# Second homes for five of an expert quad's twelve weight units, loops over two quads

## The reference, cut to what matters

```python
def hier_moe(hn, w_grp, w_exp, w_gate, w_up, w_down):
    ...
    e_in = jnp.einsum('ng,nge->ne', jax.nn.one_hot(grp, N_GROUPS, dtype=jnp.float32), e_logits)
    top_p, top_i = lax.top_k(jax.nn.softmax(e_in, axis=-1), TOP_K_IN_GROUP)
    gate = p_g * top_p / jnp.sum(top_p, axis=-1, keepdims=True)
    expert = grp[:, None] * EXPERTS_PER_GROUP + top_i.astype(jnp.int32)
    ...
    def expert_block(args):
        xb, e = args
        hh = jax.nn.silu(xb @ w_gate[e]) * (xb @ w_up[e])
        return hh @ w_down[e]
```

## Time and profile before

| | us |
|---|---|
| median of 3 runs | 1954.98 |
| lowest and highest run | 1954.23, 1959.61 |
| the profiled execution, its own time | 1956.8 |
| span of the profiled execution | 1954.9 |
| busy: PE, PEld, DVE, ACT, POOL | 1732.8, 1263.4, 864.2, 627.6, 60.0 |

### The profile page before, as it was taken

One profiled execution on the slowest core, in us unless ns is written; L12 is line 12 of the kernel. 1 busy time (PEld: TensorE's weight loads), 2 busy tenths in 40 slices (PEclk: granted clock), 3 DMA queues, 4 the chain that ended last, 5 costly groups with the idle time before them and its releaser, 6 DMA issues.

```text
span 1954.9 us, 31288 instructions
## 1 busy us (share of the span) xinstructions
PE 1732.8 (89%) x12626; PEld 1263.4 (65%) x12626; DVE 864.2 (44%) x1528; ACT 627.6 (32%) x1021; POOL 60.0 (3%) x58
## 2 busy tenths in 40 slices
PE   7999778788788899988878888899999989999997
PEld 7985334344245768543433433599888979998897
DVE  5642122122125644212212212469876555987654
ACT  4421111111113642201101111364447554543763
POOL 0200000000000010000000000100001200000110
PEclk9999998898898999988989989999999999998999
DMA  7638999999998313899999999544522334442222
GB/s 299 235 149 344 421 422 421 421 422 421 421 421 346 127 44 151 358 421 421 421 421 422 421 421 422 206 166 135 191 88 102 103 117 149 154 172 103 93 89 106
DMA packets 73091, 526.35 MB, mean 269 GB/s; under 512 B 8241, under 2 KB 8497, under 8 KB 9265
## 3 DMA queue, kind: packets, MB, share of 16 engines
q1 hardware_dynamic: 73008, 525.18, 67.3%
HBM read 524.10 MB, written 1.05 MB: 269 GB/s over the span
## 4 chain that ended last, share of the span: by engine, by line
PE 52%; DMA 27%; DVE 8%; SPq 7%; ACT 3%; issue 2%; POOL 0%; DVEq 0%; ACTq 0%
DMA arena<-experts 19%; PE banks L453 13%; PE banks L457 10%; PE banks L458 9%; PE banks L459 9%; SPq L412 7%; DMA ring<-experts 5%; PE banks L612 4%; PE banks L597 3%; PE banks L630 3%; DMA ring<-dense 2%; DVE arena L1429 2%; DVE ring_parts L1409 1%; DVE hT L1560 1%; ACT ring_parts L1016 1%
## 5 line engine op out<-in xcount | busy, mean ns | idle before, releaser
L457 PE MATMUL banks<-arena_parts,ring_parts 128*128 128x256 f32 (+1 forms) x1444 | 426.0, 295 | 28.0 <-DVE arena_parts L1424 13.2
L458 PE MATMUL banks<-arena_parts,ring_parts 128*128 128x256 f32 (+1 forms) x1444 | 415.1, 287 | 0.0
L459 PE MATMUL banks<-arena_parts,ring_parts 128*128 128x256 f32 (+1 forms) x1444 | 414.9, 287 | 0.0
L453 PEld LDWEIGHTS banks<-arena 128*128 128x128 f32 (+3 forms) x2704 | 342.9, 201 | 76.8 <-issue 60.9
L453 PE MATMUL banks<-arena 128*128 128x128 f32 (+5 forms) x2704 | 378.7, 298 | 13.4 <-DVE arena L1555 5.0
L1016 ACT ACTIVATE arena<-banks 128x256 f32<-128x256 f32 (+9 forms) x350 | 159.3, 485 | 462.4 <-PE banks L453 205.6
L457 PEld LDWEIGHTS banks<-arena_parts,ring_parts 128*128 128x128 f32 x1444 | 279.1, 193 | 39.5 <-issue 18.3
L1409 DVE TENSOR_TENSOR ring_parts<-ring,ring_parts 128x1024 fp32r<-128x1024 f32 x204 | 244.1, 1238 | 125.8 <-ACT ring_parts L1016 123.9
L612 PE MATMUL banks<-ring,arena 128*32 128x512 f32 x1536 | 210.3, 656 | 94.3 <-DMA ring<-experts 90.9
L458 PEld LDWEIGHTS banks<-arena_parts,ring_parts 128*128 128x128 f32 x1444 | 280.2, 194 | 0.1
L459 PEld LDWEIGHTS banks<-arena_parts,ring_parts 128*128 128x128 f32 x1444 | 279.5, 194 | 0.0
(11 more groups left out here) (208 smaller groups left out, 1614.2 us busy)
## 6 DMA issues: line engine op xcount, KB each, us to landing
ring<-experts SPq DMA_DIRECT2D x192, 1024.0 KB, 26.2
arena<-experts SPq DMA_DIRECT2D x160, 1024.0 KB, 20.8
ring<-dense SPq DMA_DIRECT2D x112, 1024.0 KB, 4.9
at<-experts SPq DMA_DIRECT2D x32, 1024.0 KB, 22.8
consts<-consts_in SPq DMA_DIRECT2D x1, 1414.0 KB, 13.7
vecs<-vecs_in SPq DMA_DIRECT2D x1, 1125.5 KB, 16.1
hT<-h_in SPq DMA_DIRECT2D x2, 544.0 KB, 4.6
out<-x SPq DMA_DIRECT2D x4, 256.0 KB, 2.3
```

What stands on the lines that cost most here:

```text
L453: return pe.matmul(o, lhsT, rhs, start=(k == 0), stop=(k == n - 1))
L457: pe.matmul(o, lhsT[0], rhs[0], start=(k == 0), stop=False)
L458: pe.matmul(o, lhsT[0], rhs[1], start=False, stop=False)
L459: return pe.matmul(o, lhsT[1], rhs[0], start=False, stop=(k == n - 1))
```

## The change

Units 7 to 11 get a second home, which the odd quads of a layer use; units 0 to 6 keep one home. Three of the second homes are floats 0 to 6144 of `arena`, unit 11's is floats 6144 to 8192 (over the start of `mo_n`), unit 10's is `x2`. SP issues units 7 to 11 of quad 1 right behind units 0 to 5 of quad 0, during the routing; unit 10 waits for `lg_done`, unit 11 (and what follows it in the list) for `xr_done`. From then on SP goes by turns: units 0 to 6 of quad j + 1, each when quad j has used it, then units 7 to 11 of quad j + 2, each when quad j has used it and when quad j + 1's has landed. At the end the order differs: units 0 to 6 of the last quad come before its units 7 to 11. The loops of SP and TensorE have two quads in a turn; VectorE computes the numbers for them with two more small operations; VectorE's and ScalarE's loops still go quad by quad.

```diff
+TWICE = 7
@@
-        n_iter = sb("n_iter", [P, 2], I32)
+        n_iter = sb("n_iter", [P, 4], I32)
@@
+        second_slots = arena[:, 0:4 * UNIT].rearrange("p (s n) -> p s n", n=UNIT)
+
+        def expert_slot(u, odd=False):
+
+            if odd and u >= TWICE:
+                return x2_flat[:, 0:UNIT] if u == 10 else second_slots[:, 3 if u == 11 else u - TWICE, :]
             if u < RING:
                 return ring[:, u, :]
             return more_slots[:, u - RING, :] if u < QU - 1 else at_flat[:, :]
@@
-        a = Place(3 * DC * T)
+        a = Place(4 * UNIT)
         g_squares, root_x = a(DC, P), a(SEQ)
@@
                 experts_first(layer, range(RING))
+                sp.wait_ge(pr_done, 8 * layer + 8)
+                for u in range(TWICE, QU):
+                    if u == 10:
+                        sp.wait_ge(route["lg_done"], layer + 1)
+                    if u == 11:
+                        sp.wait_ge(route["xr_done"], layer + 1)
+                    sp.wait_ge(m[f"landed{u}"], 16)
+                    sp.dma_start(expert_slot(u, True), experts[layer, 1, u]).then_inc(m[f"landed{u}"], 16)
+
+                def is_used(pair, odd, u):
+
+                    sp.wait_ge(m["used"], pair * (2 * QU) + (odd * QU + u + 1))
+
+                def next_quad(pair, odd):
+
+                    for u in range(TWICE):
+                        is_used(pair, odd, u)
+                        sp.dma_start(expert_slot(u), experts[layer, (pair * 2 + (odd + 1 + QUADS)) % QUADS, u]).then_inc(m[f"landed{u}"], 16)
+
+                def quad_but_one(pair, odd):
+
+                    for u in range(TWICE, QU):
+                        is_used(pair, odd, u)
+                        sp.wait_ge(m[f"landed{u}"], (pair * 2 + (odd + 2)) * 16)
+                        sp.dma_start(expert_slot(u, odd == 1), experts[layer, (pair * 2 + (odd + 2)) % QUADS, u])\
+                          .then_inc(m[f"landed{u}"], 16)
+
                 sp.wait_ge(route["iter_ready"], layer + 1)
-                last = sp.value_load(n_last[0:1, layer:layer + 1], min_val=QUADS - 1, max_val=QUADS * ROUNDS - 1)
+                last = sp.value_load(n_last[0:1, layer:layer + 1], min_val=QUADS // 2 - 2, max_val=QUADS * ROUNDS // 2 - 2)
                 with sp.Fori(0, last) as i:
-                    for u in range(QU):
-                        sp.wait_ge(m["used"], i * QU + (u + 1))
-                        sp.dma_start(expert_slot(u), experts[layer, (i + 1) % QUADS, u]).then_inc(m[f"landed{u}"], 16)
+                    for odd in range(2):
+                        next_quad(i, odd)
+                        quad_but_one(i, odd)
+                next_quad(last, 0)
+                quad_but_one(last, 0)
+                next_quad(last, 1)
+                next_quad(last + 1, 0)
+                quad_but_one(last, 1)
@@
-                with pe.Fori(0, n) as i:
+                def quad(i, odd):
...
-                        return expert_slot(u).rearrange("p (e n) -> p e n", e=4)
+                        return expert_slot(u, odd).rearrange("p (e n) -> p e n", e=4)
...
-                combine(n)
+
+                with pe.Fori(0, half) as pair:
+                    quad(pair * 2, False)
+                    quad(pair * 2 + 1, True)
+                combine(half * 2)
@@
-                ts(r_c, r_n, -1.0, ALU.add)
+                ts(r_c, r_n, 0.5, ALU.mult)
+                t.link(v.tensor_copy(n_iter[:, 2 + layer:3 + layer], r_c))
+                ts(r_c, r_c, -2.0, ALU.add)
                 t.link(v.tensor_copy(n_last[:, layer:layer + 1], r_c))
                 t.link(v.tensor_copy(n_iter[:, layer:layer + 1], r_n), route["iter_ready"])
```

More of the change, by code:

```diff
@@ L413, in load_experts @@
+                next_quad(last, 0)
[3 more added lines that the diff above has]
+                quad_but_one(last, 1)
                 for u in range(QU):
-                    use = (m["used"], last * QU + (u + 1))
+                    use = (m["used"], last * (2 * QU) + (3 * QU + u + 1))
                     if u < RING:
@@ L601, in moe @@
                 pe.wait_ge(route["iter_ready"], layer + 1)
-                n = pe.value_load(n_iter[0:1, layer:layer + 1], min_val=QUADS, max_val=QUADS * ROUNDS)
-                with pe.Fori(0, n) as i:
+                half = pe.value_load(n_iter[0:1, 2 + layer:3 + layer], min_val=QUADS // 2, max_val=QUADS * ROUNDS // 2)
+                def quad(i, odd):
                     def weights(u):
                         pe.wait_ge(s[f"landed{u}"], i * 16 + 16)
-                        return expert_slot(u).rearrange("p (e n) -> p e n", e=4)
+                        return expert_slot(u, odd).rearrange("p (e n) -> p e n", e=4)
                     pe.wait_ge(s["xs_ready"], i + 1)
@@ L625, in moe @@
                     pe.wait_ge(s["ht_ready"], i + 1)
-                    for half in range(2):
+                    for half_ in range(2):
                         for k in range(2):
-                            w = weights(8 + 2 * half + k)
+                            w = weights(8 + 2 * half_ + k)
                             for e in range(4):
-                                m = pe.matmul(psum[32 * e:32 * e + 32, 4 + half, :], mo_ht[:, k, 32 * e:32 * e + 32], w[:, e, :],
+                                m = pe.matmul(psum[32 * e:32 * e + 32, 4 + half_, :], mo_ht[:, k, 32 * e:32 * e + 32], w[:, e, :],
                                               start=(k == 0), stop=(k == 1), tile_position=(0, 32 * e))
                             m.then_inc(s["used"], 1)
-                combine(n)
+                with pe.Fori(0, half) as pair:
+                    quad(pair * 2, False)
+                    quad(pair * 2 + 1, True)
+                combine(half * 2)
             def mla():
```

2 lines of the change are left out of this document (1 added, 1 removed).

## The result

| | before | changed |
|---|---|---|
| median of 10 runs, us | 1958.8 | 1948.2 |
| profiled execution: own time, span | 1956.8, 1954.9 | 1945.9, 1943.9 |
| ratio, 95% interval | | 0.9948 (0.9932 to 0.9964) |
| busy PE, PEld, DVE, ACT | 1732.8, 1263.4, 864.2, 627.6 | 1730.5, 1256.7, 866.1, 627.4 |

The changed kernel is 0.52% faster, 10.2 us of 1958.8 (7.1 to 13.3). Forecast were 13.1 us and 1942, range 1936 to 1950. One of the ten executions of the changed kernel took 2010.8 us at a granted clock of 0.82 (the other nine 0.92 to 0.94); it is in the median of the table and not in the ratio. Single executions of one kernel lie 1% apart here (before: 1948.8 to 1968.6 in 30 runs of a later group), so what follows reads stages within traces.

The account below looks back on a forecast made before the run. The prediction took the 421 GB/s stream of expert weights, with a hole in each routing, to bound the kernel. Gains of 5.2 and 7.9 us made 13.1, from 1954.98 to 1942 us; its own range 1939 to 1944, overall 1936 to 1950.

Parts of the forecast that it names:

- What bounds the kernel: Both layers of experts: a stream of 1 MB units at the DMA's full rate, 421 GB/s, 2.49 us a unit.
- The hole: Expert weight stream rests during each layer's routing, 8.9 and 9.5 us; five preloaded units, 12.4 us of stream, close it.
- The end order: Layer ends: TensorE's work on the last two quads exceeds 19.9 us of stream, so layer 0 gains 4.9 to 5.8, not 8.9.
- Its size: Gain at the layer ends: 5.2 us in layer 0 (4.9 to 5.8), 7.9 in layer 1 (7.1 to 8.9).
- the one for unit 6, unit 7 and the rest of quad 14: TensorE late in each layer: unit 6 0.86 to 1.80 us, then to quad 15 16.24 (layer 0), 15.31 to 16.24 (layer 1).
- The full clock behind a quad that did not wait: Layer 1, `prep` to last `combine`: 15.58 us instead of 16.32, 0.7 us gained.
- VectorE's operations, the waits of SP, the branch: Routing and expert loops: operations and SP's waits cost nothing; branch gone between quads 14 and 15, below 0.1 us either way.
- The doubled body: TensorE's expert loop, two quads in a turn: cost taken as nothing.
- its rival at 0.06: TensorE's doubled loop body is fetched again at each of 7 turns back; at 16 us each, 1976 us; chance 0.06.
- The sum: Whole kernel: 5.2 us from layer 0 plus 7.9 from layer 1, 13.1 us gained.
- The time itself: Whole run: 1954.98 - 13.1 = 1941.9, rounded to 1942 us; range 1936 to 1950.

Follow-up runs that it names:

- hole_back: Changed kernel with the five preloads waiting until TensorE has used unit 0 of quad 0; experts 971.8 us, ratio to before 1.0042.
- last_quad_late: Changed kernel with units 7 to 11 of quad 15 issued before its units 0 to 6; experts 971.5 us, ratio to before 1.0040.
- two and four units: Two runs: end_swapped with only units 10 and 11, or units 8 to 11, preloaded; experts 957.5 and 948.9 us, ratios to before 0.9951 and 0.9926.
- end_swapped: Changed kernel with units 0 to 6 of quad 14 issued before its units 7 to 11; experts 949.1 us, ratio to before 0.9921.
- two_in_a_turn: Kernel before with only TensorE's loop doubled and VectorE's two more operations; experts 966.1 us, ratio to before 1.0008.
- four_units_preloaded: end_swapped with only units 8 to 11 given two homes and preloaded, unit 7 not; experts 948.9 us, ratio to before 0.9926.
- fillers in the waits: end_swapped with one useless matmul ahead of each of units 4 to 7 in every odd quad; experts 947.7 us, ratio to before 0.9915.

## Why the prediction was right, point by point

- **What bounds the kernel.** Right. The ends of the layers move with the stream and with which unit comes last (hole_back, last_quad_late), 2.49 us a unit.
- **The hole, 8.9 and 9.5 us, closed by five units with 3.5 and 2.9 us to spare.** Right, by the 419 and 421 GB/s and by two and four units: four (9.95 us) still close it.
- **The end order takes part of it back, since TensorE needs longer for two quads than 19.9 us.** Right: no wait on DMA in quad 15's first phase, waits back and 2.4 us gained with end_swapped, hole_back 5.4 us above before (4 to 6 expected). The moments agree once the earlier start of the stages is taken out: `prep` at 589.36 + 1.65 = 591.0 and 1218.74 + 4.58 = 1223.3, said were 591 to 592 and 1223 to 1225; quad 14 ends at 584.0 and 1216.3, said were about 585 and 1217.
- **Its size.** Gains of 5.96 and 8.96 us against 5.2 and 7.9, at or just over the upper bounds of 5.8 and 8.9. The term that was mis-sized is the one for unit 6, unit 7 and the rest of quad 14: I took a value near the lowered clock in layer 0 and the middle in layer 1 (about 17.7 and 17.2 us from the landing of unit 6 to the start of quad 15), and it was 582.38 - 565.61 = 16.77 and 1211.76 - 1195.59 = 16.17. The clock had come up again by the time unit 7 ran: both units took 2.46 and 1.86 us.
- **The full clock behind a quad that did not wait, 0.7 us in layer 1.** Right: from `prep` to the last `combine` 1234.19 - 1218.74 = 15.45 us, before 16.32.
- **VectorE's operations, the waits of SP, the branch: nothing.** Right. VectorE still waits 4.00 us for `prep(1)` (4.29 before); the stream runs at 421 GB/s from 170 to 585 us.
- **The doubled body: nothing, its rival at 0.06.** Right by two_in_a_turn.
- **The sum.** 13.1 forecast, 10.2 (7.1 to 13.3) measured. It counted nothing outside the experts. There some 4 us were lost by the traces, and 1.8 us more than forecast were gained inside (14.9 against 13.1); the two hid each other in part, and so far the nearness of the total is luck. Putting the outside at no change was the weak step: the same stages vary by 6 to 7 us in one kernel and by 14 over all versions.
- **The time itself.** 1948.2 against 1942, in the range but near its upper end. 3.8 us of the 6.2 come from the starting point: the forecast went from a median of three runs, 1954.98, and ten runs of the same kernel gave 1958.8.

## What to carry to other kernels

Where a stream bounds a loop, a second buffer is worth the hole that it fills and not the bytes that it holds: measure the hole first (rate times time of a window), here 9 us for five units of 2.49. Then look at what the new order makes land last: one changed line at the end of a layer (last_quad_late) turned 14.9 us of gain in the stages of experts into a loss of 5.1. And compare stages between marks of the same event in both traces; the whole run hid 1 to 4 us that the stages showed at once.

## What the runs showed of the hardware

- Waiting can cost twice. Among the last quad's waits on DMA the granted clock is 0.66 in a window of 7.4 us (end_swapped, layer 0: the level of 1.2 GHz for most of it), and the work behind it is slower too (`prep` 6.44 against 5.62 us). It need not: in layer 0 of four_units_preloaded the clock stayed at 1.00 through waits of 1.4 us and `prep` took 5.62 us, and in layer 1 of end_swapped, with the same waits, 6.14. With fillers in the waits the clock was 1.00 in both layers.
- Executions of one kernel differ in the time outside the experts by 6 to 7 us (983.2 to 989.5; 987.4 to 994.0). Over the traces 0.36 to 0.44 us of it go with each us that TensorE spends at the lower clock (fits through four traces of before and through all fourteen).
- The stream of 1 MB transfers held 421 GB/s for 400 us and more, with 10 or so of them in the queue (25.88 us from an issue to its landing, at 2.49 us a unit), from one issuing engine.
